# Retention and state-space scan of a hybrid block: where the mean is taken out, how scores share the array, and the order of a few waits

## The reference

```
seg = a_cum[:, :, :, None] - a_cum[:, :, None, :]
decay = jnp.exp(jnp.where(causal, seg, -jnp.inf))
cb = jnp.einsum('bclgn,bcsgn->bclsg', cm, bm)
y_diag = jnp.einsum('bclsgh,bcsghp->bclghp', cb[..., None] * decay, xdt)
...
y = y_diag + y_off + xs * d_skip.astype(F32).reshape(SSM_GROUPS, hg, 1)
y = y.reshape(b, s, BRANCH_WIDTH) * jax.nn.silu(z.astype(F32))
```

```
y = head_norm((y_inner + y_cross).reshape(b, s, RET_HEADS, RET_V_DIM), EPS)
y = y.reshape(b, s, BRANCH_WIDTH) * norm_w.astype(F32)
return (jax.nn.silu(g.astype(F32)) * y).astype(out_dtype)
```

## Time and profile before

| what | value |
|---|---|
| median of 3 runs | 3943.0 us (3940.33 to 3945.11) |
| the profiled execution | 3940.84 us, of which the span 3939.0 us |
| PE busy | 3744.2 us, 95% of the span |
| DVE, ACT, POOL busy | 2151.7, 1489.5, 99.9 us |
| Mamba scan, 692.0 to 788.1 us | PE busy 71.66 of 96.10 us |
| retention's scores, 1177 to 1211 us | PE busy 33.04 of 34 us |
| retention's norm, 1257 to 1286 us | PE busy 23.26 of 29 us |

### The profile page before, as it was taken

How to read it: one execution, slowest core, us unless ns; L and a number is a source line. 1 busy time by engine, 2 the same in 40 slices (tenths; PEclk the granted TensorE clock), 3 DMA queues, 4 the chain that set the end, 5 groups by cost and what they waited for, 6 DMA issues and landing times.

```text
span 3939.0 us, 52040 instructions
## 1 busy us (share of the span) xinstructions
PE 3744.2 (95%) x22082; PEld 3011.6 (76%) x22082; DVE 2151.7 (55%) x3213; ACT 1489.5 (38%) x2555; POOL 99.9 (3%) x128
## 2 busy tenths in 40 slices
PE   8999899799999999999989999999998999999998
PEld 6688588686876777877767887888777778878886
DVE  6855645656443566567565545434665655454346
ACT  5733333145322344343355323223433553232233
POOL 0022000100000000000001000000000010000000
PEclk9999999899999999999999999999998999999999
DMA  4100123022331222323200233232232002332322
GB/s 140 59 3 4 60 91 102 11 96 70 105 109 43 86 86 83 104 85 105 87 1 17 70 96 100 91 101 90 94 101 66 1 17 88 99 100 88 104 87 80
DMA packets 90956, 297.52 MB, mean 76 GB/s; under 512 B 10083, under 2 KB 12643, under 8 KB 90212
## 3 DMA queue, kind: packets, MB, share of 16 engines
q1 hardware_dynamic: 88848, 286.50, 22.7%
q10 hardware_dynamic: 1876, 7.71, 0.5%
HBM read 292.07 MB, written 2.10 MB: 75 GB/s over the span
## 4 chain that ended last, share of the span: by engine, by line
PE 80%; DVE 12%; ACT 5%; issue 1%; POOL 0%; DMA 0%; SPq 0%; DVEq 0%; ACTq 0%
PE ps L626 21%; PE ps L628 20%; PE ps L627 20%; PE ps L1204 2%; PE ps L1185 2%; DVE wlo L2058 2%; ACT whi L1340 2%; DVE ftm L2074 2%; PE ps L1195 1%; PE ps L765 1%; PE ps L649 1%; PE ps L651 1%; PE ps L650 1%; PE ps L770 1%; PE ps L758 1%
## 5 line engine op out<-in xcount | busy, mean ns | idle before, releaser
L2058 DVE TENSOR_TENSOR wlo<-wraw,whi 128x1024 fp32r<-128x1024 f32 (+5 forms) x603 | 664.1, 1103 | 1277.8 <-ACT whi L1340 1272.5
L1340 ACT ACTIVATE whi<-wraw 128x1024 fp32r<-128x1024 f32 (+5 forms) x603 | 577.9, 959 | 1276.8 <-PE ps L628 1193.3
L626 PE MATMUL ps<-HH,whi 128*128 128x512 f32 x1880 | 746.2, 397 | 11.1 <-DVE HL L2639 4.7
L627 PE MATMUL ps<-HL,whi 128*128 128x512 f32 x1880 | 734.1, 390 | 0.0
L628 PE MATMUL ps<-HH,wlo 128*128 128x512 f32 x1880 | 734.1, 390 | 0.0
L626 PEld LDWEIGHTS ps<-HH,whi 128*128 128x128 f32 x1880 | 354.5, 189 | 95.7 <-DVE HL L2639 8.1
L627 PEld LDWEIGHTS ps<-HL,whi 128*128 128x128 f32 x1880 | 354.5, 189 | 78.6 <-issue 5.8
L628 PEld LDWEIGHTS ps<-HH,wlo 128*128 128x128 f32 x1880 | 354.3, 188 | 74.9
L626 PE MATMUL ps<-HBh,whi 128*128 128x512 f32 x816 | 323.5, 396 | 8.8 <-DVE HBl L2639 6.3
L628 PE MATMUL ps<-HBh,wlo 128*128 128x512 f32 x816 | 319.2, 391 | 0.0
L627 PE MATMUL ps<-HBl,whi 128*128 128x512 f32 x816 | 318.9, 391 | 0.0
(11 more groups left out here) (628 smaller groups left out, 6177.7 us busy)
## 6 DMA issues: line engine op xcount, KB each, us to landing
wraw<-in_w_ff SPq DMA_DIRECT2D x88, 512.0 KB, 3.5
wraw<-in_w_bg SPq DMA_DIRECT2D x48, 512.0 KB, 3.4
wraw<-in_ffn_up SPq DMA_DIRECT2D x44, 512.0 KB, 3.2
wraw<-in_w_z SPq DMA_DIRECT2D x36, 512.0 KB, 3.2
wraw<-in_w_gate SPq DMA_DIRECT2D x32, 512.0 KB, 3.3
wraw<-in_w_br SPq DMA_DIRECT2D x32, 512.0 KB, 3.3
wraw<-in_w_rw SPq DMA_DIRECT2D x26, 512.0 KB, 3.3
wraw<-in_w_mam SPq DMA_DIRECT2D x24, 512.0 KB, 3.2
```

The source lines that it names most:

```text
L626: MM(b[0:m, :], hi[:, k, c0:c0 + m], x[0], start=(start and k == 0), stop=False)
L627: MM(b[0:m, :], hi[:, k, c0:c0 + m], x[1], start=False, stop=False)
L1340: ACTV(W.pair_of(n)[0], W.raw_of(n), ACT.Copy).then_inc(*up("act", "whi", n))
L2058: TT(l, W.raw_of(n), h.bitcast(F32), SUB).then_inc(*up("dve", "wlo", n))
```

## The change

In the scan:
- PE's transposes of dt and of the decay sums, and DVE's copies of them, come after projection tile 16 and not after tile 23; the exponential `ea` comes after the first chunk's other exponentials; the meeting of all engines at the end of "mb" becomes waits for single results.
- DVE does the clip of group g before the product (`decayed`) of group g-1.
- D*x is made by ACT in eight copies with a scale at the end of its part of each chunk, and not by POOL.

In the retention:
- DVE evicts the values from PSUM, not ACT: a sum over each head's 128 columns, a scaling with -1/128 and an addition. As the weights of the sum over tokens don't depend on the column, centred values give a centred result, so the mean matmuls and the subtraction go.
- Keys are kept as four full tiles, two heads in each; two matmuls over 64 rows each (upper and lower half) replace two over 128 rows. Score steps go by pairs of heads, scores two steps ahead of values, with six buffers for the weighted scores.
- Squares are taken from PSUM as each head is finished, and their sums are matmuls inside the score stage (six) and after the first gate tile (two); root, reciprocal and the splitting of its result in two parts of reduced float32 stand between the first gate tiles; the factor is spread by one matmul for each head over 48 rows in reduced float32, where there were two passes over 128 rows, from gate tile 2 on.

The diff, cut to its core:

```diff
+            RQ, RK = tiles(sb(c1, "rq", 4 * S)), tiles(sb(c1, "rk2", 4 * S))
+            VRr, VR2, RSEL, RM = sb(c1, "VRr", S), sb(c1, "VR2", S, dt=F32R), sb(c1, "rsel", 16, dt=F32R), sb(c1, "rvm", 32)
+            RG = RQ + RK
...
+                    if j != 16:
+                        continue
+                    for i, src in enumerate((DT, AC)):
-                for s in due("pe", *ends("mb")):
+                for s in due("pe", ("act", "xbc", 15)):
...
-                    for s in due("pe", ("dve", "rp", i), ("act", "rv1", 3)):
+                def scores(p, jb):
+                    n, banks = S - 128 * jb, [bank("rs", 2 * p + i, jb) for i in range(2)]
+                    for s in due("pe", ("dve", "rope", "rqk", 7)):
+                    for i, lo, sl in halves:
+                        MM(banks[i][:, 0:n], RK[p][sl, 128 * jb:128 * jb + 128], RQ[p][sl, 128 * jb:S], start=True,
+                           stop=True).then_inc(*up("pe", "rs", 2 * p + i, jb))
+
+                def values(p, jb):
+                    n = S - 128 * jb
+                    for h in (2 * p, 2 * p + 1):
+                        by = bank("ry", h, hold=True) if jb == 0 else PS.slots[PS.at["ry", h]]
+                        for s in due("pe", ("dve", "rp", h, jb), ("dve", "rv1", 3)):
+                        MM(by[:, 128 * jb:S], RV[:, jb, 128 * h:128 * h + 128], rpb[2 * (4 * p + jb) % 6 + h % 2][:, 0:n],
+                           start=(jb == 0), stop=(jb == 3)).then_inc(*up("pe", "ry", h, jb))
+                        if jb == 3:
+                            PS.let("ry", h)
...
-                for h in range(8):
-                    MM(b, C("ones"), Yt[h], start=True, stop=True).then_inc(*up("pe", "rm", h))
...
+                def y_norm(h):
+                    b = bank("rn", h)
+                    for s in due("pe", ("dve", "rvl")):
                         pe.wait_ge(*s)
-                    MM(b, row(h), VRr, start=True, stop=True).then_inc(*up("pe", "rn", h))
+                    MM(b, RSEL[0:48, h:h + 1].to_broadcast([48, 128]), VR2[0:48, :], start=True,
+                       stop=True).then_inc(*up("pe", "rn", h))
+                steps = [(p, jb) for p in range(4) for jb in range(4)]
+                for t in range(16 + 2):
+                    if t < 16:
+                        scores(*steps[t])
+                    if t >= 2:
+                        values(*steps[t - 2])
+                    if t >= 8 and t % 4 == 0 and t < 17:
+                        y_sum(t // 2 - 4)
+                        y_sum(t // 2 - 3)
+                here("pe", "end", "rs")
+                for j in range(8):
+                    tile(("rg", j), "w_ret", (8 + j,), 8, H, hn)
+                    if j == 0:
+                        y_sum(6)
+                        y_sum(7)
+                    if j >= 2:
+                        y_norm(j - 2)
+                y_norm(6)
+                y_norm(7)
...
-                for need in due("act", *ends("mb")):
-                    act.wait_ge(*need)
+                    if c == 0:
+                        for need in due("act", ("dve", "dtT", 1)):
+                            act.wait_ge(*need)
+                        ACTV(ea, acT, ACT.Exp).then_inc(*up("act", "ea"))
+                    for need in due("act", ("pe", "xd", c, 1)):
+                        act.wait_ge(*need)
+                    for j in range(8):
+                        ins = ACTV(xs3[:, j, 128 * c:128 * c + 128], xs3[:, j, 128 * c:128 * c + 128], ACT.Copy,
+                                   scale=P("ssm_d", j))
+                    ins.then_inc(*up("act", "dx", c))
...
-                    for c in range(4):
-                        evac(("rv%d" % g, c), RV[:, c, 512 * g:512 * g + 512], ACT.Copy, ("rv%d" % g, c))
                 for h in range(8):
-                    for need in due("act", ("pe", "ry", 4 * h + 3)):
-                        act.wait_ge(*need)
+                    for need in due("act", ("pe", "ry", h, 3), ("pe", "rsq", h - 4) if h >= 4 else None):
+                        act.wait_ge(*need)
+                    ACTV(rtm[h % 4], PS.of("ry", h), ACT.Square).then_inc(*up("act", "rsq", h))
                     ACTV(Yt[h], PS.of("ry", h), ACT.Copy).then_inc(*up("act", "ry", h))
-                for need in due("act", *ends("rs")):
-                    act.wait_ge(*need)
-                for h in range(8):
-                    for need in due("act", ("dve", "rm", h), ("pe", "rsq", h - 4) if h >= 4 else None):
-                        act.wait_ge(*need)
-                    ACTV(rtm[h % 4], Yt[h], ACT.Square).then_inc(*up("act", "rsq", h))
-                ACTV(VRr[0:16, :], PL[0:16, :], ACT.Sqrt, bias=EPSC[0:16], scale=1.0 / 128).then_inc(*up("act", "rvr"))
+                    if j == 0:
+                        for need in due("act", ("pe", "rsq", 7), ("dve", "vr1")):
+                            act.wait_ge(*need)
+                        ACTV(VRr[0:16, :], PL[0:16, :], ACT.Sqrt, bias=EPSC[0:16], scale=1.0 / 128).then_inc(*up("act", "rvr"))
+                    if j == 1:
+                        for need in due("act", ("dve", "rvr")):
+                            act.wait_ge(*need)
+                        ACTV(VR2[0:16, :], VRr[0:16, :], ACT.Copy).then_inc(*up("act", "rvh"))
...
+                    for i, dst in enumerate((dtT, acT) if j == 0 else ()):
+                        for need in due("dve", ("pe", "dtT", i)):
+                            dve.wait_ge(*need)
-                for need in due("dve", *ends("mb")):
+                for need in due("dve", ("dve", "dtT", 1)):
+
+                    def decayed(g):
+                        for need in due("dve", ("act", "seg", c, g), ("dve", "cb", c)):
+                            dve.wait_ge(*need)
+                        TT(r3(MMt[g], 128), r3(MMt[g], 128), bmid(CB[:, 128 * g:128 * g + 128], 4),
+                           MUL).then_inc(*up("dve", "M", c, g))
+                        for need in due("dve", ("pe", "seg", c, g), ("pe", "yd", c - 1, g // 2) if c else None):
-                        for need in due("dve", ("act", "seg", c, g)):
-                            dve.wait_ge(*need)
-                        TT(r3(M, 128), r3(M, 128), bmid(CB[:, 128 * g:128 * g + 128], 4), MUL).then_inc(*up("dve", "M", c, g))
+                        if g:
+                            decayed(g - 1)
+                    decayed(3)
+                    for need in due("dve", OWN):
+                        dve.wait_ge(*need)
...
-                            for need in due("dve", ("pe", "yo", c, hf)):
+                            for need in due("dve", ("pe", "yo", c, hf), ("act", "ea")):
-                        for need in due("dve", ("pe", "yk", c, hf), ("pool", "dx", c)):
+                        for need in due("dve", ("pe", "yk", c, hf), ("act", "dx", c)):
...
-                    dst = [(slice(0, 128), RQ[j])] if j < 4 else [
-                        (slice(64 * i, 64 * i + 64), KPr[2 * (j - 4) + i][64 * i:64 * i + 64, :]) for i in range(2)]
-                    rope("rqk", j, ("rsw", j), dst, Dc[8], Dc[9], rtm, ("act", "rqk", j))
+                    rope("rqk", j, ("rsw", j), [(slice(0, 128), RG[j])], Dc[8], Dc[9], rtm, ("act", "rqk", j))
...
+                    for c in range(4):
+                        key, m = ("rv%d" % g, c), RM[:, 16 * g + 4 * c:16 * g + 4 * c + 4]
+                        for need in due("dve", ("pe", *key)):
+                            dve.wait_ge(*need)
+                        RED(m, r3(PS.of(*key), 128), AXX, ALU.add).then_inc(*up("dve"))
+                        for need in due("dve", OWN):
+                            dve.wait_ge(*need)
+                        TS(m, m, -1.0 / 128, None, MUL).then_inc(*up("dve"))
+                        for need in due("dve", OWN):
+                            dve.wait_ge(*need)
+                        TT(r3(RV[:, c, 512 * g:512 * g + 512], 128), r3(PS.of(*key), 128), bc(m, 128),
+                           ADD).then_inc(*up("dve", *key))
+                        PS.free(key, ("dve", *key))
+                        for h in (2 * p, 2 * p + 1):
+                            for need in due("dve", ("pe", "rs", h, jb),
+                                            ("pe", "ry", 2 * ((t - 3) // 4) + h % 2, (t - 3) % 4) if t >= 3 else None):
+                                dve.wait_ge(*need)
+                            TT(rpb[2 * t % 6 + h % 2][:, 0:n], PS.of("rs", h, jb)[:, 0:n], Dc[h][:, 0:n],
+                               MUL).then_inc(*up("dve", "rp", h, jb))
+                            PS.free(("rs", h, jb), ("dve", "rp", h, jb))
-                for h in range(8):
-                    for need in due("dve", ("pe", "rm", h)):
-                        dve.wait_ge(*need)
+                def normed(h):
                     for need in due("dve", ("pe", "rn", h), ("act", "rg", h)):
                         dve.wait_ge(*need)
```

(17 more changed lines are left out.)

95 lines of the change are left out of this document (20 added, 75 removed).

## The result

The changed kernel takes 3920.28 us (median of 4 runs, 3918.17 to 3924.63); beside it the kernel before took 3944.02 (3940.33 to 3945.11). The ratio is 0.9943, 95% interval 0.9926 to 0.9960: 23.7 us or 0.6% faster, where 36.5 us were forecast. The profiled execution of after took 3924.63 us, the slowest of its four; where it differs from e11, both are given.

What follows compares the result with a forecast made beforehand. PE was taken to bound the kernel, busy 3744.2 of 3939.0 us. Scan 21.8 plus retention 14.7 made 36.5 us gained; against the runs' median of 3943.0 that gave 3906.5 us, range 3892 to 3922.

Steps and rivals of the forecast that it cites:

- Start of the scan: Scan: with transposes, copies, exponential and meeting moved away, DVE's first copy comes earlier; gain 2.5 us.
- Groups: Scan: with the product one group late, three of four DVE waits for ACT vanish; 2.6 us a chunk, 10.4 in all.
- D*x: Scan: eight ACT copies replace POOL's work, so DVE's waits for POOL in chunks 0 to 2 mostly go; gain 8.9 us.
- Next late there: Scan, after a 21.8 us gain: DVE, nearly without a gap, and PE at low clock would be late next; no size given.
- Rival A: Scan clock stays at 1.00, some 4 us more there and 4 in the retention; 3898 us, chance 0.15.
- Values: Retention: DVE's evictions make PE lose 2.2 us at the second group and start the first value products 5.8 us late.
- Clock of the retention: Retention: low PE clock behind two pauses of 3.9 and 7 us costs 1.6 to 2 us each, 3.6 us here.
- Pairs: Retention scores: two heads' 64-row matmuls overlap, with 0.20 us lost before the next 128-row product; gain 4.5 us (0 to 8.6).
- Norm: Retention: the 32.0 us norm tail gives way to 7.2 us of sums and 3.0 of broadcasts, root beside gate tiles; gain 21.8 us.
- B: Retention gives little: pairs don't overlap, evictions at upper bound, late root, clock low longer; 3921 us, chance 0.15.
- C: Slower: PE's clock stays at half in both the score stage and the scan; 3974 us, chance 0.03.
- D: No change: PE waits for the split behind the gate tiles and centring eats the rest; 3942 us, chance 0.05.

Runs made afterwards that it cites:

- e11: The changed kernel measured a second time with no edit; 3918.05 us.
- e1: The kernel before with only the scan part of the change; 3924.01 us.
- e7: The changed kernel with idle-time 128x128 matmuls into an unread bank behind the decay matmuls of the scan's chunks; 3911.51 us.
- e10: The changed kernel with matmuls into an unread bank where PE waits in the retention (second value projection, first three score steps); 3911.16 us.
- e5: The changed kernel with keys padded with zeros to 128 rows again, one head per score matmul; 3917.80 us.
- e2: The kernel before with only the retention part of the change; 3934.32 us.

## Why the prediction was right, and where it was not

Right in direction and inside the range. The size was off by 12.8 us (11.5 with both sets), so the outcome that was given 0.62, a time within 8 us of 3906.5, did not come: 3920.28 lies 13.8 above. One error went in the kernel's favour, 1.0 us for the groups; the others went against it, and the large ones are prices of pauses and of changes of rows that were too low or missing. By its own steps:

**Start of the scan.** Forecast 2.5 us. From PE's last projection matmul to DVE's first copy it was 6.7 us before (691.9 to 698.56) and is 4.3 now (695.20 to 699.49): 2.4.

**Groups.** Forecast 2.6 us a chunk. Four groups with their products take 7.22 us (718.56 to 725.78), where four of the earlier trace rows take 10.08: 2.86 a chunk, 11.4 in all. The last group's product stands behind the third's without a wait (timeline of DVE, after; first copy, last two products, the line behind them):

```profile
718.56 0.15 DVE L2480 COPY TK<-ps 128x4 f32<-128x4 f32 x1
...
724.27 1.47 DVE L2473 TENSOR_TENSOR MM<-MM,CB 128x512 f32<-128x512 f32 x2
725.78 0.17 DVE L2491 TENSOR_TENSOR TK<-TK 128x16 f32<-128x16 f32 x1
```

**D*x.** Forecast 8.9 us, with 1.6 us of ACT for eight copies and an upper bound of 4.8. They take 2.43, and the waits of the earlier trace rows are 0.16 or nothing. The 8.9 us of waits went as forecast. Timeline of after, ACT's copies in chunk 0 and DVE's first use of them:

```profile
707.30 2.43 ACT L1642 ACTIVATE XS<-XS,PT 128x128 f32<-128x128 f32 x8
...
714.10 0.69 DVE L2532 TENSOR_TENSOR mtmp<-ps,XS 128x512 f32<-128x512 f32 x1 [0.16 <-PE ps L945]
```

**"Next late there: DVE itself ... and PE where its clock is low."** This is the step of the scan that failed. The terms as measured make 2.4 + 11.4 + 8.9 = 22.7 us and the stage gave 17.7 (19.2 in e1, 20.8 in e11). I named the low clock and gave it no price. Its price is DVE's wait for line 926, up from 1.0 to 5.0 us in after (4.3 in e1, 2.3 in e11), and e7 gives 5.0 back (72.2 us, where seven profiles with the same scan have 75.4 to 78.5, 77.2 on average). Rival A had this the wrong way round: the clock did not rise by itself with shorter chunks.

**Values.** Forecast a wait of 3.9 us in place of 1.69, measured 4.00. Forecast first products with values 5.8 us later, measured 5.9 (from the first score 9.34 us, 1166.90 to 1176.24, where it was 3.41). Both are right. Timeline of PE in after: the second group's start, then the first three score steps:

```profile
1142.07 0.79 PE L647 MATMUL ps<-whi,HH 128*128 128x512 f32 x1 [4.00 <-DVE rv L2628]
...
1166.90 1.13 PE L991 MATMUL ps<-rq,rk 64*128 64x512 f32 x4
1170.96 0.92 PE L991 MATMUL ps<-rq,rk 64*128 64x384 f32 x4 [2.94 <-DVE rv L2628]
1174.11 1.23 PE L991 MATMUL ps<-rq,rk 64*128 64x256 f32 x4 [2.23 <-DVE rv L2628]
```

**Clock of the retention.** Forecast 3.6 us for two pauses, measured 2.9 + 2.9 = 5.8. The two groups of values took 51.2 us in place of 46.0, of which 2.3 is the wait. The first pair's two products and one score step took 6.70 us (1176.24 to 1182.94), where the second pair's take 3.82 at full clock (1187.18 to 1191.00). e10, which gives back 5.7 against this profile, agrees. In e11 the same two terms are 1.7 and 2.4, together 4.1, and e10 gives back 4.0.

**Pairs.** Forecast 4.5 us, from the first product with values on. At full clock a pair of heads takes 8.06 us where two heads took 8.64, so 2.3 for four pairs, and about 0.7 more by score work that now lies in the pause: 29.3 us at full clock (3.82, three times 8.06, and 1.33 for the last two products) where before had 32.4, a gain of 3.0. The loss on the way out of the half rows was missing from the sum. The stage as measured, without six sums of squares, is 32.2 us, so the half clock of the term above took 2.9 of this back. e5 bears it out: against full rows the edit gave 0.4 to 0.9 us here.

**Norm.** Forecast 21.8 us, measured 20.1 (from the end of the score stage to the end of the last broadcast 75.5 us before and 49.9 now, less 5.5 for six sums that moved ahead of it). The broadcasts took 4.3 us (five of 0.64 and three in 1.1) and not 3.0, and the sums of squares 7.5 and not 7.2: that is 1.6 of the missing 1.7. Root and reciprocal stood beside gate tiles as worked out: DVE's rest ended at 1231.4, PE wanted it at 1232.49, a slack of 1.1 us where one was forecast.

**Retention.** -2.3 - 5.9 - 5.8 + 3.0 + 20.1 = 9.1 us for 14.7, which is the difference of the stages in the table (197.3 to 188.2; 10.8 with the 186.5 us of e11 and e2). e2 gave 8.8 for the kernel. So of the 11.5 us missing, 2.7 (e1) lie in the scan and 5.9 (e2) in the retention; the remaining 3 no experiment places, and they are within the intervals.

**Rivals.** B's number, 3921 us, is the measured one, but by coincidence: a part of the shortfall is the scan's, for which B had nothing. Two of its ingredients are there in part (losses of the row changes 1.5 us for 5, the clock low for longer 2.2 for 4); the dear evictions and the late root are not. C's mechanism exists, but the clock came back within 4 to 12 us at both places of the retention. D fell: both merges are full. What stays open is why the unchanged stages differ by 3 to 5 us between profiles.

## What to carry to other kernels

A pause of PE of 3 us can cost more than 3 us: here the clock halved behind such pauses, and the next engine then waited for PE. Price it with the pause. Where the pause can't be moved, cheap matmuls into an unused bank bought 3 to 6 us of the stage here at each of two places (7 to 8 by the medians). Removing one of two waits in a loop may give much less than its length (3.6 and 6.0 us here by the medians, the earlier start included) where removing both gives 16. Evictions belong where the next work does not depend on them: moving two projections by a few tiles gave 14 to 16 us of the stage (19 by the medians), more than any other edit.

## What the runs showed of the hardware that I had not expected

- The length of one pause doesn't tell whether the clock falls. In after it stayed at 2.4 GHz behind 1.01 us (chunk 1) and fell to 1.2 in the chunks with pauses of 1.44, 2.99 and 2.72 us (0, 2 and 3). In e7 the same pauses of 0.98 and 0.57 us stand in chunk 2, where it stayed, and, as 0.97 and 0.56, in chunk 3, where the eight passes of line 921 took 1.79 us and not 1.10. Which execution gets which was not settled.
- A change between 128 rows and fewer costs about 0.2 us in each direction, for float32 scores on 64 rows (0.40 for both) and for a reduced float32 broadcast over 48 rows, which takes 0.64 us between two tiles where the same over 128 takes 0.26.
- An ACT copy of 128x128 in SBUF with a scale for each partition takes 0.30 us in a row of eight (2.43/8); the copies from PSUM without one took 0.20. No run tells whether the scale or the memory makes the difference.
